# Eighteen of the 22 feed-forward units of a two-layer block: from eight block products each to the seven of Strassen's identity

## The reference

```python
def swiglu(h, w_gate, w_up, w_down):
    return (jax.nn.silu(h @ w_gate) * (h @ w_up)) @ w_down
# for l in 0, 1, twice in each layer, with gains of their own:
h = rms_norm(x, gn[0])
x = x + 0.5 * rms_norm(swiglu(h, w_ffn1_gate[l], w_ffn1_up[l], w_ffn1_down[l]), gn[1])
```

## Time and profile before

| | us |
|---|---|
| median of three runs | 2921.28 |
| the profiled execution, whole | 2916.3 |
| its span, first to last instruction | 2914.5 |
| PE busy in the span | 2821.4 |
| DVE busy | 1452.9 |
| ACT busy | 1056.2 |
| POOL busy | 107.4 |

### The profile page before, as it was taken

One profiled execution on the slowest core, in us unless ns is written; L12 is line 12 of the kernel. 1 busy time (PEld: TensorE's weight loads), 2 busy tenths in 40 slices (PEclk: granted clock), 3 DMA queues, 4 the chain that ended last, 5 costly groups with the idle time before them and its releaser, 6 DMA issues.

```text
span 2914.5 us, 38312 instructions
## 1 busy us (share of the span) xinstructions
PE 2821.4 (97%) x14920; PEld 1498.1 (51%) x14920; DVE 1452.9 (50%) x2109; ACT 1056.2 (36%) x1530; POOL 107.4 (4%) x107
## 2 busy tenths in 40 slices
PE   8999999999999999999999999999999899998998
PEld 5444476654544445444566654544455454554553
DVE  4333375646533334333476546433255665456644
ACT  4222265442422233222455543322243444335342
POOL 0000012100000000000022000000000010000010
PEclk9999999999999999999999999999999999999999
DMA  5333312222333342333322324233333121321212
GB/s 155 101 101 112 112 59 66 84 69 94 98 102 102 98 127 71 102 99 99 115 66 66 102 73 123 72 101 97 112 102 102 58 73 58 103 75 58 73 58 80
DMA packets 324996, 263.62 MB, mean 90 GB/s; under 512 B 25164, under 2 KB 288588, under 8 KB 324464
## 3 DMA queue, kind: packets, MB, share of 16 engines
q1 hardware_dynamic: 322608, 254.57, 28.9%
q10 hardware_dynamic: 1632, 4.95, 0.6%
q0 software_dynamic: 608, 2.11, 0.2%
HBM read 257.40 MB, written 4.21 MB: 90 GB/s over the span
## 4 chain that ended last, share of the span: by engine, by line
PE 76%; issue 7%; DVE 6%; ACT 5%; DMA 2%; DVEq 2%; POOL 1%; ACTq 1%; SPq 0%; POOLq 0%
PE pu L447 14%; PE pu L449 14%; PE pu L448 14%; PE pm L447 9%; PE pm L449 9%; PE pm L448 9%; PE pm L824 2%; DVE w_lo L999 1%; POOL arena L1880 1%; PE pm L838 1%; ACT w_hi L1577 1%; DMA stage<-in_w_ffn_up_dram 1%; PE pm L653 1%; DVE small L1388 1%; DMA stage<-in_w_in_dram 1%
## 5 line engine op out<-in xcount | busy, mean ns | idle before, releaser
L999 DVE SCALAR_TENSOR_TENSOR w_lo<-stage,w_hi 128x2048 f16<-128x2048 f32 x228 | 519.0, 2276 | 422.2 <-ACT w_hi L1577 414.6
L447 PE MATMUL pu<-h_hi,w_hi 128*128 128x512 f16 x1488 | 570.1, 383 | 9.5 <-DVE tb L1078 3.4
L449 PE MATMUL pu<-h_hi,w_lo 128*128 128x512 f16 x1488 | 569.6, 383 | 0.0
L448 PE MATMUL pu<-h_lo,w_hi 128*128 128x512 f16 x1488 | 569.6, 383 | 0.0
L1577 ACT ACTIVATE w_hi<-stage 128x2048 f16<-128x2048 f32 (+1 forms) x139 | 261.4, 1881 | 473.2 <-PE pm L449 381.2
L447 PEld LDWEIGHTS pu<-h_hi,w_hi 128*128 128x128 f16 x1488 | 148.7, 100 | 188.6 <-issue 20.3
L447 PE MATMUL pm<-h_hi,w_hi 128*128 128x512 f16 x640 | 242.6, 379 | 0.0
L448 PE MATMUL pm<-h_lo,w_hi 128*128 128x512 f16 x640 | 242.6, 379 | 0.0
L449 PE MATMUL pm<-h_hi,w_lo 128*128 128x512 f16 x640 | 242.6, 379 | 0.0
L449 PEld LDWEIGHTS pu<-h_hi,w_lo 128*128 128x128 f16 x1488 | 146.8, 99 | 179.3 <-issue 6.8
L448 PEld LDWEIGHTS pu<-h_lo,w_hi 128*128 128x128 f16 x1488 | 146.8, 99 | 169.6 <-issue 8.2
(11 more groups left out here) (277 smaller groups left out, 4081.8 us busy)
## 6 DMA issues: line engine op xcount, KB each, us to landing
stage<-in_w_in_dram SPq DMA_DIRECT2D x136, 512.0 KB, 4.5
stage<-in_w_ffn_gate_dram SPq DMA_DIRECT2D x88, 512.0 KB, 3.9
stage<-in_w_ffn_up_dram SPq DMA_DIRECT2D x88, 512.0 KB, 5.1
stage<-in_w_ffn_down_dram SPq DMA_DIRECT2D x80, 512.0 KB, 3.9
stage<-in_w_out_dram SPq DMA_DIRECT2D x40, 512.0 KB, 4.6
stage<-in_w_in_dram SPq DMA_DIRECT2D x24, 256.0 KB, 3.2
stage<-in_w_ffn_down_dram SPq DMA_DIRECT2D x16, 256.0 KB, 4.1
stage<-in_w_branch_hgrn_dram SPq DMA_DIRECT2D x8, 512.0 KB, 3.5
```

Of the source, the lines that this page charges most:

```text
L447: nc.tensor.matmul(ps, w1, r_hi, start=first, stop=False)
L448: nc.tensor.matmul(ps, w1, r_lo, start=False, stop=False)
L449: return nc.tensor.matmul(ps, w2, r_hi, start=False, stop=last)
L999: V.scalar_tensor_tensor(out=w_lo[:, s, 0:n], in0=stage[:, s, 0:n], scalar=WSCALE, in1=w_hi[:, s, 0:n], op0=ALU.mult, op1=ALU.subtract).th ...
```

## The change

Of the 22 units the first four stay as they were, units 2 and 3 now in the text ahead of the loop and in the *other* set of banks. The 18 units after them (a loop of nine steps of two, `FAST` = 18) take the unit as a product of 2 x 2 blocks: the tokens in two halves of 256 (`HT`), the 1024 rows of `h` in a low and a high half of four k blocks, and the unit's columns as up and gate. Strassen's identity in Winograd's form makes the four block results from seven block products. A block product is 4 k blocks by 3 matmuls of 256 columns: 84 matmuls of 256 columns a unit. It needs

- four mixed forms of `h` (`h_forms`, `tf_hi_t`, `tf_lo_t`), made once for each FFN: 12 DVE instructions of 1024 elements a partition and four casts on ACT, after `h` is complete;
- four sums of the unit's weight blocks (`weight_sums`, 512 elements each), fp32, then split in high and low like the three blocks that are used as they are (`direct`, `high_sums`, `low_direct`, `low_sums`): 3584 elements to split in place of 2048;
- partial results taken from PSUM in the middle of a unit by ACT (`grab`, four of 256 columns, on `prod`, answered by `copied`), because PE goes on adding to the same bank, and five 256-wide DVE instructions that put the four results together (`gate_second`, `gate_first`, `up_second`, two in `gated`).

The cast to `a_hi` moves from DVE to ACT. A unit uses three banks in place of two. The banks of an FFN's halves are exchanged throughout (`set_a` for `set_b`), and up and gate change places in a slot. PE waits `forms_ready` within unit 3. The core of the diff:

```diff
+PLAIN = 4
+FAST = KF - PLAIN
+        sc = f32(53, 8, HT)
+        sums = f32(61, 8, HD)
+        form = [f32(61 + 4 * i, 4, HT) for i in range(4)]
+        tf_hi_t, tf_lo_t = f16(77, 16, HT), f16(85, 16, HT)
@@ tensor
+                pe.wait_ge(split, t.next("split"))
+                pe.wait_ge(evac, t.next("evac"))
+                part(alpha, gate_low, low(tok0), True).then_inc(prod, 1)
+                part(beta, gate_high, high(tok0), True)
+                pe.wait_ge(split_s, t.next("split_s"))
+                pe.wait_ge(copied, t.next("copied"))
+                part(alpha, s2, mixed(1), False).then_inc(prod, 1)
+                part(gamma, s1, mixed(0), True).then_inc(prod, 1)
+                pe.wait_ge(copied, t.next("copied"))
+                part(alpha, s3, mixed(2), False).then_inc(prod, 1)
+                pe.wait_ge(copied, t.next("copied"))
+                part(gamma, s4, high(tok1), False)
+                pe.wait_ge(copied, t.next("copied"))
+                part(alpha, up_high, mixed(3), False).then_inc(unit_done, 1)
 ...
                 first_units(banks, up_at, old, xn)
-                with pe.Fori(0, KF // 2 - 1) as j, t.steps(j, KF // 2 - 1, dict(split=2, evac=2)):
+                for s in range(2):
+                    pe.wait_ge(split, t.next("split"))
+                    t.next("evac")
+                    for k in range(KD):
+                        if (s, k) == (1, KD - 1):
+                            pe.wait_ge(forms_ready, t.next("forms_ready"))
+                        last = in_step(old[2 * s:2 * s + 2], s, up_at(k), k)
+                    last.then_inc(unit_done, 1)
+                with pe.Fori(0, FAST // 2) as j, t.steps(j, FAST // 2, dict(split=2, evac=2, split_s=2, copied=8)):
                     for s in range(2):
+                        fast_unit(s, (banks, old)[s][0:3])
@@ vector
+            def weight_sums(s):
+                v.wait_ge(land[s], t.next(f"land{s}", 32))
+                V.tensor_tensor(s1, up_low, up_high, ALU.add)
+                V.tensor_tensor(s3, gate_low, up_low, ALU.subtract)
+                v.drain()
+                V.tensor_tensor(s2, s1, gate_low, ALU.subtract)
+                v.drain()
+                V.tensor_tensor(s4, gate_high, s2, ALU.subtract).then_inc(s_ready, 1)
 ...
                 lo(1)
+                h_forms()
                 for s in range(2):
-                    up_evac(banks, bass.ds(s, 1), s)
+                    plain_evac(banks, bass.ds(s, 1), s)
+                v.drain()
+                weight_sums(0)
+                plain_evac(old, bass.ds(2, 1), 0)
+                low_direct(0)
+                low_sums(0)
+                weight_sums(1)
+                plain_evac(old, bass.ds(3, 1), 1)
+                low_direct(1)
+                gate_first(0, sets[0])
+                low_sums(1)
+                up_second(0)
+                def step(s, f):
+                    gate_second(1 - s, sets[1 - s])
+                    weight_sums(1 - s)
+                    gated(1 - s, sets[1 - s])
+                    low_direct(1 - s)
+                    gate_first(s, sets[s])
+                    low_sums(1 - s)
+                    up_second(s)
+                    gated_low(1 - s, f)
@@ scalar
+                def step(s, f, plain=False):
+                    s_.wait_ge(land[1 - s], t.next(f"land{1 - s}", 32))
 ...
+                        s_.wait_ge(unit_done, t.next("unit_done"))
+                        direct(1 - s, 512, 1280)
+                        silu(1 - s)
+                    grab(s, alpha, 0)
+                    direct(1 - s, 1280, 2048).then_inc(hi_split, 1)
+                    high_sums(1 - s, 0, 1)
+                    grab(s, alpha, 1)
+                    high_sums(1 - s, 1, 4)
+                    grab(s, gamma, 3)
+                    grab(s, alpha, 2)
+                    if not plain:
+                        gated_high(1 - s, f)
```

More of the change, by code:

```diff
@@ L1084, in ffn @@
             def ffn(banks, old, gain):
+                sets = banks[0:3], old[0:3]
                 lo(1)
+                h_forms()
                 for s in range(2):
-                    up_evac(banks, bass.ds(s, 1), s)
[L1088 to L1091, removed]
+                    plain_evac(banks, bass.ds(s, 1), s)
@@ new lines, in ffn @@
+                with v.Fori(0, FAST // 2 - 1) as j, t.steps(j, FAST // 2 - 1, dict(unit_done=2, land0=32, land1=32, act_done=2, hi_split=2, copied=8,
+                                                                                   s_split=2, ah_ready=2)):
+                    step(1, bass.ds(j * 2 + PLAIN, 1))
+                    step(0, bass.ds(j * 2 + PLAIN + 1, 1))
+                for s in range(2):
+                    f = bass.ds(KF - 2 + s, 1)
+                    gate_second(s, sets[s])
+                    gated(s, sets[s])
+                    lo(s, DOWN[s] * HD)
+                    if s == 0:
+                        gate_first(1, sets[1])
+                        up_second(1)
+                    gated_low(s, f)
@@ new lines, in high_sums, with grab @@
+                def high_sums(s, first, last):
+                    e_hi = first_w[s][0]
+                    if first == 0:
+                        s_.wait_ge(s_ready, t.next("s_ready"))
+                        A.activation(w_hi[:, s, 0:512], sums[:, 4 * s], ACT.Copy, scale=WSCALE)
+                    if last == 4:
+                        A.activation(e_hi[:, 0:1536], sums[:, 4 * s + 1:4 * s + 4].rearrange("p a b -> p (a b)"), ACT.Copy, scale=WSCALE).then_inc(s_split, 1)
+                def grab(s, bank, i):
+                    s_.wait_ge(prod, t.next("prod"))
+                    A.activation(sc[:, 4 * s + i], bank[:, 0:HT], ACT.Copy).then_inc(copied, 1)
@@ L1663, in ffn @@
                 hi_after_tail()
+                for i in (0, 2, 1, 3):
+                    s_.wait_ge(tf_ready, t.next("tf_ready"))
+                    A.activation(tf_hi_t[:, 4 * i:4 * i + 4], form[(1, 2, 0, 3)[i]], ACT.Copy).then_inc(tf_hi, 1)
                 for s in range(2):
[L1665 to L1670, removed]
+                    gate_act(banks, s)
```

199 lines of the change are left out of this document (160 added, 39 removed).

## The result

The changed kernel takes 2838.4 us (median of four executions, 2837.3 to 2839.7), the one before 2922.2 beside it (2914.0 to 2923.4): a ratio of 0.9719 with a 95% interval of 0.9701 to 0.9738, or 84 us less. The forecast was 2852, from 69 us less. The profiled executions are 2916.3 before and 2839.7 after, spans 2914.5 and 2837.9: 76.6 less. The other 7 us of the 84 come from which execution was profiled: that of before lay 6 under its median, that of after 1 above. What must be explained is 76.6 against 69.

The account below looks back on a forecast made before the run. PE's matmul stream was taken as the bound: 17 units x 1.18 = 20.0 us an FFN, less losses at the starts, together 69 us; from the median 2921.3 that gives 2852 us, range 2838 to 2875.

Parts of the forecast that it names:

- PE's part: Fast unit on PE: 84 matmuls of 256 columns take 9.18 us against 10.36 before, 1.18 us less a unit.
- the rival of a slower 256-wide stream: Fast units: 256-wide matmuls start 0.111 us or more apart, 12 us per 0.002; 2860 to 2885, chance 0.06.
- DVE's step: DVE's work for one fast unit, summed by distances of starts: 9.06 us, 0.12 less than PE's 9.18.
- DVE is the bound: Rival, fast loop: DVE's step takes more than 9.18 us, up to 9.93; time 2875 to 2905, chance 0.19.
- The first rival: Fast loop: DVE's step exceeds PE's unit, 68 x 0.75 = 51 us more at 9.93; chance 0.19.
- Waits inside a unit: Fast unit: ACT and DVE deliver in time; PE stalls only if DVE is over about 0.4 us late.
- The starts: Start of each FFN: DVE's 27.4 us chain delays unit 4; losses 3.5 in FFN 0, 5.2 in FFN 2.
- Program fetch: Rival, loop branches: PE refetches its program at each branch back, 198 us, less 69: 3050; with other repeated stalls, chance 0.13.
- The end: Down units behind the fast loop: free, the second having 7.8 us to cover unit 21's evacuation and the next split.
- The sum: All four FFNs: 16.5 in FFN 0, 19 in FFN 1 and 3, 14.8 in FFN 2, together 69 us.
- The range: Whole kernel: 2838 to 2875 us, from no start stalls and best pace to a DVE step of 9.5; chance 0.62.

Follow-up runs that it names:

- the version with six plain units: The changed kernel with units 4 and 5 of FFN 0 and 2 also computed directly, evacuations put ahead of and between the forms: 2832.2 us, repeated 2832.6.

## Why the prediction was right, point by point

- *PE's part*, 9.18 us a unit: 9.17 in the steady loop. The columns came off the end, 1.19 us for each unit. With 0.1092 us from start to start, the rival of a slower 256-wide stream (0.111 or more) is out.
- *DVE's step*, 9.06: measured 8.94. The mechanism was right (starts, not lengths, add up, through semaphore waits and the branch), the size 0.12 off: 13 instructions and 2 drains, each term put some 0.01 too high. The slack is 0.23 and not 0.12. It changed nothing in the time, as PE was the bound either way, but the chance of 0.19 for "DVE is the bound" came from that thin margin. The slope was one for one in each step that DVE bounds, but these are 15 an FFN and not 17: 6.0 us for each 0.1 and not 6.8. The first rival's price was too high by that eighth.
- *By the Trainium skill* (VectorE: DVE Perf Modes, "The DRAIN you can't avoid") the next instruction does not start until the pipe is empty, from which the prediction took that the lengths would add. The trace does not agree: 0.61 us from start to start for an instruction 0.68 long, with a met wait between, and a whole step of 8.94 against 9.93. The same section of the Trainium skill goes on that an instruction which is not held starts earlier, which the prediction left out; with that the trace agrees.
- *Waits inside a unit*: none in the steady loop, as worked out.
- *The starts*: the chain 27.9 us, forecast 27.4 (0.2 too little each for the forms with the wait behind them, for the first two evacuations and for `low_direct`); idle 7.3 and 5.3, forecast 6.6 and 4.1; in FFN 1 and 3 0.7, forecast 0.2. This was the step most under-sized, by 0.5 to 1.2 us each, and the version with six plain units shows that nothing else holds PE there. The half clock behind it cost 2.2 and 2.6, forecast 2.8. In FFN 1 and 3 the waits on `sc` in the first fast units came to 0.7, forecast 0.9 and 0.6.
- *Program fetch*: refuted at both body lengths. The 11 blocks more of the longer text are fetched once an FFN and not once a pass. Of the two statements of the Trainium skill (Runtime: NRT & Kernel Launch, "Instruction fetch mechanics") the buffer of 2048 instructions agrees with a body of about 1,050 that stays, and the rule on branches out of two pages does not.
- *The end*: free. PE shows no wait in the first 20 us behind the loop, in any of the four FFNs.
- *The sum*: the four FFNs gave 71.4 us, forecast 69. Of the 13.6 us between forecast and median, 2.4 lie there, and 5.2 in "all else", a difference of two executions that the repeated kernel shows to be within the spread of one program. The last 6 are that spread again: the profiled execution of before, 5 under the median that the 69 were taken off, and that of after, 1 above its own.
- *The range*: the median, 2838.4, lies on its very edge (2838 to 2875). The low end was meant for no stall at the starts and the best pace; the stalls came, longer than forecast. The mechanism is right within 2.4 us in the FFNs, but the range left out how far executions of one program lie apart (2828 to 2849), and that the median fell inside it is luck.

## What to carry to other kernels

Where one engine's stream is the bound and another is about to become as loaded, count the second engine's step by starts and not by lengths, and then measure its slack by adding an instruction of known width: the distance of a repeated instruction tells 0.01 us where the time of the program can't tell 5. A transformation with a set-up (here the forms) needs enough of the old work ahead of it to cover the set-up on the engine that does it. And run the unaltered kernel again beside the variants before explaining a few microseconds.

## What was not expected of the hardware

Behind a gap of 2.3 us in PE's stream 16 matmuls went at half pace (granted clock 0.50), after nine at full pace (0.98). Behind gaps of 0.4 to 0.7 us there were none. How many there are does not follow the length of the gap: behind 7.1 us there were some 13 with the longer loop body and 28 with the added 256-wide instruction, behind the 4.7 us of FFN 2 in the changed kernel's second trace some 28. So the 2.2 and 2.6 us lost at the starts are themselves good to within 0.8 us or so. And one program on one core spread over 2828 to 2849 us, in step with its mean granted clock (0.992 to 0.985); the two of its executions that have traces, 2840 and 2828, agree in their FFN lengths within 0.3 us.
